# Attention with three score buffers, outputs in their free columns, and the grouped heads four jobs at a time with V stationary

## The chip, the cores and the metric

The kernel runs on one core of a Trainium2 chip. The metric is the device time of one execution in microseconds (us). The kernel before took 1500.85 us in the median of three runs (1499.09 to 1501.25).

## The reference

The reference is one layer of a diffusion backbone for 512 latent tokens and 128 prompt tokens of width 1024. What is touched here is the attention of two kinds of heads and the projections right behind it:

```python
def diff_attention(q, k, v, lam, lambda_init, subln_g):      # A: 8 heads, two maps each
    s = jnp.einsum('bqhnd,bkhnd->bhnqk', qb, k) * scale
    p = jax.nn.softmax(s, axis=-1)
    a = p[:, :, 0] - lam * p[:, :, 1]
    o = jnp.einsum('bhqk,bkhe->bqhe', a, v)
    o = rms_norm(o, subln_g) * (1.0 - lambda_init)
def gqa_attention(q, k, v):                                  # B: 16 query heads, 4 key/value heads
    s = jnp.einsum('bqhgd,bkhd->bhgqk', qg, k) * scale
    o = jnp.einsum('bhgqk,bkhd->bqhgd', jax.nn.softmax(s, axis=-1), v)
merged = sigmoid(ga) * (o_a @ w_br_a) + sigmoid(gb) * (o_b @ w_br_b)
x = ln_affine(alpha * x + g1 * (merged @ w_o), ...)
```

Latent queries attend to 640 keys (512 latent and 128 cached ones), prompt queries to the 128 prompt keys. Behind it come a router, an expert layer with two experts a token, and a second norm.

## The kernel before, in words

The kernel is written with five hand-ordered instruction streams, one for each engine, that meet at semaphores. Every engine works its own stream strictly in the order of the program. The stages are: modulation and the combined projection (to about 485 us), the attention (to about 811 us), the branch and output projections, the router, the experts, and the last norm.

**The attention.** A job is one tile of 128 queries with one head; its number is j. Heads come in 12 bundles: 8 of kind A (5 jobs, one for each query tile, two score maps a job) and 4 of kind B (4 query heads that share keys and values, times 5 tiles, one map a job), together 120 jobs and 160 maps. A job is wide for the four latent tiles (640 keys) and narrow for the prompt tile (128 keys). A job passes these steps:

- TensorE multiplies queries and keys into a score buffer of PSUM (`scores`, L1621; matmuls on L1633). There are two score buffers, `pair[0]` and `pair[1]`, used in turn (`spair`, L385); a map waits until the exponential of the map two before is done.
- VectorE takes the negated maximum of each row (L1186), and ScalarE the exponential with its row sum into an SBUF buffer `pbuf` (L874).
- For A, VectorE forms the difference of the two maps, with the reciprocals of the sums and lambda in it (L1196 to L1198).
- TensorE turns the 128x128 blocks of P into `pair[2]` (`turn_p`, L1636, L1643). There is one such place, so the turning waits until the job before has been copied out.
- ScalarE copies the turned P to SBUF (`copy_turned`, L397, the copy on L404); for one B job in three VectorE does it (`copied_by_dve`, L394).
- TensorE multiplies the turned P, as the stationary operand, with V (`times_v`, L1646, L1656) into one of two places in `pair[3]` (`obank`, L388).
- VectorE scales the output by the reciprocal sum into a staging tile (L1209, L1213), and GpSimd's queue stores a bundle's outputs, in rows of tokens, to DRAM (L1910).

The order in which each engine meets these steps is fixed by loops over j. TensorE's loop (L1659) and ScalarE's (L864) are

```python
for j in range(NJ + 3):                       # TensorE, L1659
    if j < NJ: scores(jobs[j][4])
    if 0 <= j - 2 < NJ: turn_p(j - 2)
    if j < NJ and not jobs[j][1]: scores(jobs[j][4] + 1)
    if 0 <= j - 3 < NJ: times_v(j - 3)
for j in range(NJ + 2):                       # ScalarE, L864: exponentials of job j, then
    if 2 <= j and not copied_by_dve(j - 2): copy_turned(act, act.copy, j - 2)
```

VectorE's loop (L1180) holds, for each j: the maxima of job j, the difference of job j-1 (A), its copy of job j-2 if it has one, and the scaling of the output of job j-4. SP's queue loads queries, keys and V of the bundles ahead, with two buffers; a load of V waits until the bundle two before is through its V products.

**Behind the attention.** The outputs are read back in rows of tokens, one query tile at a time, five tiles of A and then five of B (`load_o`, L879, three places). A's are squared (`square`, L889, ScalarE), normed per head (`norm_o`, L1216, VectorE, a chain of small steps with two passes of 1024 columns) and all ten are turned by TensorE (`turn_o`, L1678, transposes on L1675). ScalarE rounds the turned rows to the high part (`round_o`, L896), VectorE takes the low part (`rest_o`, L1228), and then the branch projection of the tile runs with three passes (`three_passes`, L1691, L1695 to L1697), 20 units v of 24 matmuls. The gain of the sub-norm is loaded by GpSimd's queue after the last store, and VectorE scales it.

The modulation earlier in the kernel uses matmuls whose stationary operand has 32 columns, in four column groups in turn (L1542).

## Time and profile before

| | us |
|---|---|
| median of the runs shown | 1500.85 (1499.09 to 1501.25) |
| the profiled execution's own time | 1499.63 |
| its span, first to last instruction | 1497.4 |
| TensorE busy in the span | 1300.7 |
| VectorE busy | 989.6 |
| ScalarE busy | 649.3 |
| GpSimd busy | 171.7 |
| mean granted TensorE clock | 0.935 of 2.4 GHz |

The engines are named PE (TensorE matmuls), PEld (its weight loads, beside the matmuls), DVE (VectorE), ACT (ScalarE), POOL (GpSimd) and SP (SyncE); ACTq and the like are their DMA issues. L12 is line 12 of the kernel. Busy time does not count waiting, and an instruction's duration reaches from its start to its end, so that pipelined instructions of TensorE overlap: the distance from one start to the next says how long the engine was held. What an idle engine waited for is inferred from semaphores.

### The profile page before, as it was taken

What the parts mean: (1) busy time and instruction counts of PE and PEld (TensorE: products, weight loads), DVE (VectorE), ACT (ScalarE), POOL (GpSimd) and SP (SyncE); (2) the same over time, 40 slices, a digit from 0 to 9 for tenths busy, and PEclk for the clock granted to TensorE, in tenths of its full rate; (3) what the DMA queues carried; (4) which work ended last, traced back from release to release, by engine and by line L of the source; (5) the groups of instructions that cost most, each with busy time, mean ns of one, the idle gap of its engine ahead of it and who ended that gap; (6) DMA issues with size and microseconds to landing.
All of it is one profiled execution on the core that took longest, in us unless ns stands there. A gap on an engine that the chain in (4) does not pass through costs nothing.

```text
span 1497.4 us, 20859 instructions
## 1 busy us (share of the span) xinstructions
PE 1300.7 (87%) x6836; PEld 1063.8 (71%) x6836; DVE 989.6 (66%) x1814; ACT 649.3 (43%) x962; POOL 171.7 (11%) x236
## 2 busy tenths in 40 slices
PE   6899999999999778799986799996389999999940
PEld 3677777667887667788886688785368888888830
DVE  3655521838561777755555844499689999999936
ACT  2422222323222566545553322200357888888812
POOL 0012111111122000000000000100101121112201
PEclk9799999999999899999998799997589999999975
DMA  9856554453535676602202434436489999999834
GB/s 354 268 183 218 190 211 162 155 183 102 183 134 172 160 181 173 172 26 61 80 19 69 160 121 137 146 137 243 166 301 354 364 383 388 391 391 375 312 149 70
DMA packets 144419, 301.05 MB, mean 201 GB/s; under 512 B 18972, under 2 KB 24636, under 8 KB 144344
## 3 DMA queue, kind: packets, MB, share of 16 engines
q1 hardware_dynamic: 122104, 232.19, 45.1%
q0 software_dynamic: 20800, 62.63, 13.1%
q10 hardware_dynamic: 1440, 5.24, 1.1%
q8 instruction: 45, 0.74, 0.2%
q14 instruction: 30, 0.25, 0.1%
HBM read 258.69 MB, written 53.90 MB: 209 GB/s over the span
## 4 chain that ended last, share of the span: by engine, by line
PE 73%; DVE 14%; issue 6%; ACT 4%; DMA 2%; SPq 1%; POOL 0%; ACTq 0%; DVEq 0%; POOLq 0%
PE psum_pair L1556 7%; PE psum_pair L1557 7%; PE psum_pair L1558 7%; PE psum_pair L1777 5%; PE psum_pair L1778 5%; PE psum_pair L1779 5%; PE psum_pair L1695 4%; PE psum_pair L1643 4%; PE psum_pair L1696 4%; PE psum_pair L1697 4%; PE psum_pair L1656 4%; PE psum_pair L1633 4%; PE psum_pair L1792 2%; PE psum_pair L1793 2%; PE psum_pair L1794 2%
## 5 line engine op out<-in xcount | busy, mean ns | idle before, releaser
L1556 PE MATMUL psum_pair<-w_parts,h_hi 128*128 128x512 f32 x520 | 209.9, 404 | 6.3 <-DVE h_lo L1164 6.3
L1557 PE MATMUL psum_pair<-w_parts,h_hi 128*128 128x512 f32 x520 | 205.5, 395 | 0.0
L1558 PE MATMUL psum_pair<-w_parts,h_lo 128*128 128x512 f32 x520 | 205.4, 395 | 0.0
L1186 DVE TENSOR_REDUCE minus_max<-psum_pair 128x1 f32<-128x640 f32 (+1 forms) x160 | 114.3, 715 | 99.0 <-PE psum_pair L1633 98.6
L874 ACT ACTIVATE p_unnormed<-psum_pair,minus_max 128x640 f32<-128x640 f32 (+1 forms) x160 | 113.5, 709 | 144.4 <-DVE minus_max L1186 144.2
L1022 DVE TENSOR_TENSOR w_parts<-w_raw,w_parts 128x1024 fp32r<-128x1024 f32 x72 | 83.3, 1220 | 106.1 <-ACT w_parts L789 106.0
L1633 PE MATMUL psum_pair<-k_bundle,q_bundle 128*128 128x512 f32 (+1 forms) x576 | 128.4, 342 | 5.8 <-ACT p_unnormed L874 5.1
L1656 PE MATMUL psum_pair<-v_bundle,p_turned 128*128 128x64 f32 (+1 forms) x1008 | 131.3, 275 | 0.0
L1556 PEld LDWEIGHTS psum_pair<-w_parts,h_hi 128*128 128x128 f32 x520 | 99.2, 191 | 37.4 <-issue 18.3
L1656 PEld LDWEIGHTS psum_pair<-v_bundle,p_turned 128*128 128x128 f32 x1008 | 122.9, 193 | 1.4
L1558 PEld LDWEIGHTS psum_pair<-w_parts,h_lo 128*128 128x128 f32 x520 | 99.3, 191 | 21.5
L1557 PEld LDWEIGHTS psum_pair<-w_parts,h_hi 128*128 128x128 f32 x520 | 99.5, 191 | 19.0
L1633 PEld LDWEIGHTS psum_pair<-k_bundle,q_bundle 128*128 128x128 f32 x576 | 89.0, 195 | 13.8 <-issue 6.8
L1435 DVE TENSOR_TENSOR w_parts<-w_raw_b,w_parts 128x1024 fp32r<-128x1024 f32 x76 | 88.0, 1220 | 4.3 <-ACT w_parts L951 4.3
L1435 DVE TENSOR_TENSOR w_parts<-w_raw,w_parts 128x1024 fp32r<-128x1024 f32 x76 | 87.8, 1217 | 0.6 <-ACT w_hi_c L951 0.6
L1435 DVE TENSOR_TENSOR w_lo_c<-w_raw_c,w_hi_c 128x1024 fp32r<-128x1024 f32 x76 | 87.8, 1216 | 0.2 <-ACT w_hi_c L951 0.2
L789 ACT CAST w_parts<-w_raw 128x1024 fp32r<-128x1024 f32 x72 | 70.3, 1047 | 40.3 <-PE psum_pair L1697 38.1
L800 ACT ACTIVATE turned_staging<-psum_pair 128x1024 f32<-128x1024 f32 (+1 forms) x38 | 36.4, 960 | 108.0 <-PE psum_pair L1588 108.0
L951 ACT CAST w_hi_c<-w_raw_c 128x1024 fp32r<-128x1024 f32 x76 | 73.7, 1047 | 7.6 <-DVE control L1426 7.6
L1695 PE MATMUL psum_pair<-w_parts,oA_turned_hi 128*128 128x512 f32 x160 | 66.0, 413 | 9.4 <-DVE oA_turned_lo L1232 7.9
L951 ACT CAST w_parts<-w_raw 128x1024 fp32r<-128x1024 f32 x76 | 74.0, 1051 | 0.2 <-issue 0.2
L951 ACT CAST w_parts<-w_raw_b 128x1024 fp32r<-128x1024 f32 x76 | 73.9, 1053 | 0.0
(311 smaller groups left out, 2585.0 us busy)
## 6 DMA issues: line engine op xcount, KB each, us to landing
w_raw<-in_w_gate_up SPq DMA_DIRECT2D x76, 512.0 KB, 7.6
w_raw_c<-in_w_gate_up SPq DMA_DIRECT2D x72, 512.0 KB, 8.6
w_raw_b<-in_w_down SPq DMA_DIRECT2D x72, 512.0 KB, 7.7
w_raw<-in_w_in SPq DMA_DIRECT2D x52, 512.0 KB, 8.8
ada_raw<-in_w_ada SPq DMA_DIRECT2D x32, 512.0 KB, 7.1
k_bundle<-k_transposed SPq DMA_DIRECT2D x28, 384.0 KB, 8.2
q_transposed<-turned_staging POOLq DMA_DIRECT2D x20, 512.0 KB, 4.0
ada_raw_early<-in_w_ada SPq DMA_DIRECT2D x16, 512.0 KB, 8.2
```

Source lines behind the costliest of these rows:

```text
L874: act.activation(pbuf[:, m % PR, 0:w], spair(m)[:, 0:w], ACT.Exp, bias=nmax[:, m % RR:m % RR + 1], accum_out=rsum[:, m % RR:m % RR + 1]).t ...
L951: act.copy(expert_hi(place, c), landing(place, c)).then_inc(hi_done, 1)
L1022: dve.tensor_tensor(w_parts[b % 2][:, 1, c], w_raw[:, c], w_parts[b % 2][:, 0, c].bitcast(F32), ALU.subtract).then_inc(lo_done, 1)
L1186: dve.tensor_reduce(nmax[:, m % RR:m % RR + 1], spair(m)[:, 0:width(j)], AX.X, ALU.max, negate=True).then_inc(nb_done, 1)
L1435: dve.tensor_tensor(expert_lo(place, c), landing(place, c), expert_hi(place, c).bitcast(F32), ALU.subtract).then_inc(lo_done, 1)
L1556: pe.matmul(bank(n), a_hi, hi, start=first, stop=False)
L1557: pe.matmul(bank(n), a_hi, lo, start=False, stop=False)
L1558: last = pe.matmul(bank(n), a_lo, hi, start=False, stop=end)
L1633: last = pe.matmul(spair(m)[:, c0:c0 + w], q, k[:, g, k0:k0 + w], start=g == 0, stop=g == 1)
L1656: last = pe.matmul(obank(j)[:, 0:w], ptb[:, j % 2, k], vb[bi % 2][:, vt, 0:w], start=k == 0, stop=k == len(tiles) - 1)
L1695: pe.matmul(out, a_hi[:, kk], hi, start=kk == 0, stop=False)
L1777: pe.matmul(out, xt_hi[:, kk], hi, start=kk == 0, stop=False)
```

## The change

Score maps get three buffers in turn (`scores_of`). Outputs go to free columns of a score buffer: the output of a job (A) or group (B) is put behind the 640 score columns of a later map, its host, and ScalarE takes it after that map's exponential (`take_o`). In A, the V product of job j-3 is issued before the second scores of job j. In B, P is scaled by the reciprocal sum before it is turned, four jobs (two query tiles times two heads) share one V product with V as the stationary operand and 256 columns streaming, the two heads at output partitions 0 to 63 and 64 to 127, and the output comes out turned; it is stored turned and needs no transposes later. VectorE copies one B job in five instead of one in three. The read-back and first norm of A's outputs stand inside B's loops. The diff, cut:

```diff
-        pair = [... for i in range(4)]
+        psum = ctx.enter_context(nc.psum_tensor("psum_pair", [P, 8 * CW], F32))
+        pair = [psum[:, 2 * CW * i:2 * CW * (i + 1)] for i in range(4)]
...
-        for bi, (kind, _) in enumerate(bundles):
-            for r in range(REP if kind else 1):
-                for tt in range(NT):
+            together = [[(r, tt) for tt in tts for r in (2 * half, 2 * half + 1)] for half in range(REP // 2)
+                        for tts in ((0, 1), (2, 3), (PROMPT,))] if kind else [[(0, tt)] for tt in range(NT)]
...
+        for g, (_, kind, members) in enumerate(outs):
+            j = members[-1] + (4 if kind else 3)
+            host[g] = (jobs[j][4] + (0 if jobs[j][1] else 1)) if j < NJ else NM + j - NJ
+            hosted[host[g]] = g
...
-        def spair(m):
-            return pair[m % 2]
+        def scores_of(m):
+            return pair[m % SR][:, 0:NKEY]
+        def out_of_map(m, w):
+            return pair[m % SR][:, NKEY:NKEY + w]
...
         def copied_by_dve(j):
-            return jobs[j][1] == 1 and j % 3 == 0
+            return jobs[j][1] == 1 and (j - N_A) % 5 == 2
...
+            # ScalarE
+            def take_o(g):
+                act.wait_ge(pv_ready, g + 1)
+                if kind:
+                    act.copy(ost_b[:, q % 2, 0:w], out_of_map(host[g], w)).then_inc(o_out, 1)
+                else:
+                    act.activation(ost[:, bi % 2, tt], out_of_map(host[g], P), ACT.Copy,
+                                   scale=rinv[:, m % RR:m % RR + 1]).then_inc(o_out, 1)
+            for j in range(NJ + 4):
+                if j < NJ:
+                    for m in [m for m in range(jobs[j][4], NM) if maps[m][0] == j]:
...
+                        act.activation(pbuf[:, m % PR, 0:w], scores_of(m)[:, 0:w], ACT.Exp, ...
+                        if m in hosted:
+                            take_o(hosted[m])
+                if 2 <= j < NJ + 2 and not copied_by_dve(j - 2):
                     copy_turned(act, act.copy, j - 2)
+                if j == N_A + 20:
+                    for z in range(OS):
+                        load_o(z)
+                if j == N_A + 30:
+                    square(0)
+                if j == N_A + 50:
+                    square(1)
...
+            # VectorE: the maxima of job j, then for i = j - 1
+                    if kind:
+                        link(dve.reciprocal(rinv[:, s0:s0 + 1], rsum[:, s0:s0 + 1]))
+                        dve.tensor_scalar(p, p, rinv[:, s0:s0 + 1], None, ALU.mult).then_inc(a_done, 1)
+                    dve.wait_ge(a_done, i + 1)
+                i = j - 2
+                if 0 <= i < NJ and copied_by_dve(i):
+                    copy_turned(dve, dve.tensor_copy, i)
+                if j == N_A + 40:
+                    norm_o(0)
...
+            norm_o(1)
...
+            # TensorE
+            def wait_place(m):
+                if m >= SR:
+                    pe.wait_ge(e_done, min(m - SR + 1, NM))
+                    if m - SR in hosted:
+                        pe.wait_ge(o_out, hosted[m - SR] + 1)
...
+            def times_v(g):
...
+                    if kind:
+                        w = len(members) // 2 * P
+                        for half in range(2):
+                            last = pe.matmul(out_of_map(host[g], w)[HD * half:HD * half + HD], vb[bi % 2][:, vt, 0:HD],
+                                             ptb_b[:, g % 2, half, k, 0:w], start=first, stop=end)
...
-            for j in range(NJ + 3):
-                if j < NJ:
+            for j in range(NJ + 4):
+                if j < NJ and not jobs[j][1]:
                     scores(jobs[j][4])
-                if 0 <= j - 2 < NJ:
-                    turn_p(j - 2)
-                if j < NJ and not jobs[j][1]:
+                    if 0 <= j - 2:
+                        turn_p(j - 2)
+                    if 0 <= j - 3:
+                        times_v(j - 3)
                     scores(jobs[j][4] + 1)
-                if 0 <= j - 3 < NJ:
-                    times_v(j - 3)
+                else:
+                    if j - 3 < N_A:
+                        times_v(j - 3)
+                    if N_A <= j - 4 < NJ and outs[out_of[j - 4]][2][-1] == j - 4:
+                        times_v(out_of[j - 4])
+                    if j < NJ:
+                        scores(jobs[j][4])
+                    if j - 2 < NJ:
+                        turn_p(j - 2)
...
             def turn_o(z):
-                if z >= 2 * NT:
+                if z >= NT:
                     return
...
+            # GpSimd's queue, for each of B's 24 groups
+                pool.wait_ge(o_out, g + 1)
+                pool.dma_start(ot_scr[2 * bundles[bi][1] + r // 2, :, tt * P:tt * P + w], ost_b[:, q % 2, 0:w]).then_inc(ob_st[q % 2], 16)
```

B's outputs are then loaded turned (in pieces of 128 columns, 512 bytes), ScalarE rounds and VectorE splits them straight from SBUF.

## Rows read from the trace of the kernel before

**Rows 1.** Windows: length; busy PE, PEld, DVE, ACT, POOL (count); granted clock; DMA share, GB/s.

```profile
485.00:631.50 146.50, 117.11 (x803) 102.91 (x804) 112.10 (x242) 85.61 (x205) 6.57 (x8) 0.97 0.66 169
631.50:811.10 179.60, 161.60 (x1288) 149.69 (x1286) 101.07 (x265) 89.64 (x210) 3.45 (x4) 1.00 0.16 45
811.10:825.70 14.60, 1.94 (x8) 1.57 (x8) 6.38 (x20) 3.23 (x3) 3.57 (x6) 0.54 0.64 205
825.70:842.60 16.90, 10.26 (x41) 8.19 (x41) 14.72 (x34) 8.02 (x8) 0.00 (x0) 0.70 0.35 122
```

**Rows 2.** Timeline in A: start, duration, engine, line; in brackets the idle time before.

```profile
550.39 0.35 DVE L1213 TENSOR_SCALAR o_staging<-psum_pair,p_sums_recip 128x128 f32<-128x128 f32 x1
...
550.75 0.74 PE L1643 MATMUL psum_pair<-identity,p_difference 128*128 128x128 f32 x5 [0.92 <-ACT p_turned L404]
...
551.25 0.88 PE L1633 MATMUL psum_pair<-k_bundle,q_bundle 128*128 128x512 f32 x4
...
551.97 1.33 PE L1656 MATMUL psum_pair<-v_bundle,p_turned 128*128 128x128 f32 x10
552.17 0.82 DVE L1186 TENSOR_REDUCE minus_max<-psum_pair 128x1 f32<-128x640 f32 x1 [0.70 <-PE psum_pair L1633]
...
553.03 0.80 ACT L874 ACTIVATE p_unnormed<-psum_pair,minus_max 128x640 f32<-128x640 f32 x1 [0.64 <-DVE minus_max L1186]
553.05 0.42 PE L1633 MATMUL psum_pair<-k_bundle,q_bundle 128*128 128x128 f32 x2
...
553.81 0.68 ACT L404 COPY p_turned<-psum_pair 128x640 f32<-128x640 f32 x1
...
554.64 0.74 PE L1643 MATMUL psum_pair<-identity,p_difference 128*128 128x128 f32 x5 [1.17 <-ACT p_turned L404]
```

**Rows 3.** Order of instructions in B.

```profile
800.72 0.88 PE L1633 MATMUL psum_pair<-k_bundle,q_bundle 128*128 128x512 f32 x4
...
801.63 0.82 DVE L1186 TENSOR_REDUCE minus_max<-psum_pair 128x1 f32<-128x640 f32 x1 [0.91 <-PE psum_pair L1633]
...
802.49 0.80 ACT L874 ACTIVATE p_unnormed<-psum_pair,minus_max 128x640 f32<-128x640 f32 x1 [1.44 <-DVE minus_max L1186]
...
803.28 0.68 ACT L404 COPY p_turned<-psum_pair 128x640 f32<-128x640 f32 x1
...
804.11 0.73 PE L1643 MATMUL psum_pair<-identity,p_unnormed 128*128 128x128 f32 x5 [1.10 <-ACT p_turned L404]
```

**Rows 4.** Groups by shape, whole span: busy us, mean ns of one.

```profile
L874 ACT ACTIVATE p_unnormed<-psum_pair,minus_max 128x128 f32<-128x128 f32 x32 | 11.8, 368 | 19.9 <-DVE minus_max L1186 19.9
...
L1186 DVE TENSOR_REDUCE minus_max<-psum_pair 128x1 f32<-128x128 f32 x32 | 9.3, 289 | 22.0 <-PE psum_pair L1633 21.7
...
L404 ACT COPY p_turned<-psum_pair 128x128 f32<-128x128 f32 x19 | 4.9, 257 | 0.5 <-PE psum_pair L1643 0.5
...
L1153 DVE TENSOR_SCALAR x_tiles<-x_tiles,x_mean_var,x_rstd 128x1024 f32<-128x1024 f32 x5 | 3.7, 808 | 0.0
```

**Rows 5.** TensorE's order in the modulation stage.

```profile
35.99 3.64 PE L1542 MATMUL psum_pair<-ada_raw_early,cond_columns 128*32 128x512 f32 x32
```

**Rows 6.** Order behind the attention, VectorE and TensorE.

```profile
814.76 1.22 DVE L1221 TENSOR_REDUCE o_mean_squares<-o_squares 128x8 f32<-128x1024 f32 x1 [3.06 <-ACT o_squares L894]
...
818.43 1.22 DVE L1225 TENSOR_TENSOR o_rows<-o_rows,o_rms_recip 128x1024 f32<-128x1024 f32 x1
...
819.91 1.94 PE L1675 MATMUL psum_pair<-identity,o_rows 128*128 128x128 f32 x8 [8.94 <-DVE o_rows L1225]
...
875.76 1.03 PE L1675 MATMUL psum_pair<-identity,o_rows 128*128 128x128 f32 x8
876.57 0.47 PE L1695 MATMUL psum_pair<-w_parts,oB_turned_hi 128*128 128x512 f32 x1
```

**Rows 7.** Window of a stretch at the attention's start.

```profile
498.50:502.00 3.50, 3.47 (x16) 3.13 (x15) 2.00 (x4) 1.97 (x5) 0.00 (x0) 0.56 0.38 85
```

**Rows 8.** Timeline: a V pass in that stretch.

```profile
499.45 2.34 PE L1656 MATMUL psum_pair<-v_bundle,p_turned 128*128 128x128 f32 x10
```

More of the change, by code:

```diff
@@ L367, in hybrid_step @@
                     maps += [(j, 0)] if kind else [(j, 0), (j, 1)]
-        NJ, NM = len(jobs), len(maps)
-        job_end = {bi: max(j for j, q in enumerate(jobs) if q[0] == bi) + 1 for bi in range(len(bundles))}
+                    out_of.append(len(outs))
+                outs.append((bi, kind, list(range(first, len(jobs)))))
+        NJ, NM, N_OUT = len(jobs), len(maps), len(outs)
+        N_A = NT * A_HEADS
+        host, hosted = {}, {}
+        for g, (_, kind, members) in enumerate(outs):
+            j = members[-1] + (4 if kind else 3)
+            host[g] = (jobs[j][4] + (0 if jobs[j][1] else 1)) if j < NJ else NM + j - NJ
+            hosted[host[g]] = g
+        out_end = {bi: max(g for g, q in enumerate(outs) if q[0] == bi) + 1 for bi in range(len(bundles))}
         map_end = {bi: max(m for m, q in enumerate(maps) if jobs[q[0]][0] == bi) + 1 for bi in range(len(bundles))}
@@ L1632, in scores @@
                     for k0, c0, w in runs:
-                        last = pe.matmul(spair(m)[:, c0:c0 + w], q, k[:, g, k0:k0 + w], start=g == 0, stop=g == 1)
+                        last = pe.matmul(scores_of(m)[:, c0:c0 + w], q, k[:, g, k0:k0 + w], start=g == 0, stop=g == 1)
                 last.then_inc(s_ready, 1)
@@ L1649, in times_v @@
                 if bi:
                     pe.wait_ge(v_in[bi % 2], 32 * ((bi + 1) // 2))
-                if j >= 2:
-                    pe.wait_ge(o_out, j - 1)
-                tiles = [PROMPT] if tt == PROMPT else list(range(TL)) + [NT]
-                w = HD if kind else P
+                wait_place(host[g])
+                tiles = [PROMPT] if jobs[last_job][3] == PROMPT else list(range(TL)) + [NT]
                 for k, vt in enumerate(tiles):
-                    last = pe.matmul(obank(j)[:, 0:w], ptb[:, j % 2, k], vb[bi % 2][:, vt, 0:w], start=k == 0, stop=k == len(tiles) - 1)
+                    first, end = k == 0, k == len(tiles) - 1
+                    if kind:
+                        w = len(members) // 2 * P
+                        for half in range(2):
+                            last = pe.matmul(out_of_map(host[g], w)[HD * half:HD * half + HD], vb[bi % 2][:, vt, 0:HD], ptb_b[:, g % 2, half, k, 0:w], start=first, stop=end)
+                    else:
+                        last = pe.matmul(out_of_map(host[g], P), ptb_a[:, g % 2, k * P:(k + 1) * P], vb[bi % 2][:, vt, 0:P], start=first, stop=end)
@@ L1670, in _ @@
+            pe.wait_ge(o_out, N_OUT)
             pe.wait_ge(e_done, NM)
+            for i in range(2):
+                pe.wait_ge(pt_full[i], NJ // 2)
             def turn_rows(n, src):
@@ L1706, in _ @@
                 pe.wait_ge(lo_done, NC_CH * (b + 1))
[L1707 removed]
+                if v < NT:
                     pe.wait_ge(tr_free[(TR_O + v) % 2], (TR_O + v) // 2 + 1)
+                elif v < 2 * NT:
+                    pe.wait_ge(ot_done, v - NT + 1)
                 cols = slice(tt * P, (tt + 1) * P)
```

233 lines of the change are left out of this document (121 added, 112 removed).

## The prediction, made before the change was run

> **What bounds the kernel now.** I read the windows by stage first, then the order of single instructions inside the attention, because the change lives there. In the window table the attention of the differential heads (A) takes 146.5 us and that of the grouped heads (B) 179.6 us; then come 14.6 and 16.9 us in which TensorE works little before the branch projections run steadily [rows 1]. No engine is full in A: TensorE is busy 117 of 146.5 us, VectorE 112, ScalarE 86. In B TensorE is busy 162 of 180. So A must be bound by a chain, B partly.
>
> The chain in A shows in the order of instructions [rows 2]. Call J a job; a wide one has 640 keys, a narrow one (prompt) 128, in the ratio 4 to 1. The transposes of job J-2 start at 550.75. 0.50 us later TensorE starts the second score pass of J (551.25), then V of J-3 (551.97). The maximum follows its scores by 0.92 (552.17), the exponential the maximum by 0.86 (553.03), ScalarE's copy of the turned J-2 by 0.78 (553.81), and the transposes of J-1, which need that one PSUM place, by 0.83 (554.64). The sum is 3.89 us, and 554.64 - 550.75 is 3.89. The copy could run earlier, but stands behind both exponentials of J in ScalarE's queue, and the transposes wait for it. The V pass lies outside the chain: issued after the second scores, it covers TensorE's wait. With 32 wide jobs of 3.89 and 8 narrow ones at about 1.7 this makes some 138 us; the 9 left of 146.5 are the start.
>
> B has the same chain with one map a job [rows 3]: scores 800.72, maximum 801.63, exponential 802.49, copy 803.28, transposes of the job before 804.11, that is 3.39 us from the scores of J to the transposes of J-1. With 0.50 for these transposes, scores of J+2 cannot start before 3.89 plus whatever TensorE does between.
>
> **Part 1, A: V moves ahead of the second scores.** The new order on TensorE is first scores J, transposes J-2, V of J-3, second scores J. V now stands inside the chain: 551.97 to the next scores at 553.05 is 1.08 us for ten instructions [rows 2]. VectorE's scaling of the output goes; ScalarE takes the output instead, after the exponential of the hosting map and before the copy, again in the chain. The nearest row is the 128x128 copy of 0.257 us [rows 4]; its bounds are 0 (if it hid) and 0.37, the narrow exponential [rows 4]; I take 0.26, a copy of the same size. The cycle becomes 3.89 + 1.08 + 0.26 = 5.23 us. A narrow job adds 0.22 (two of ten V instructions) and 0.26. Per head 4 x 1.34 + 0.5 = 5.8 us, for eight heads **+46 us**. VectorE's saving of 0.35 a job is worth nothing, since VectorE waits for scores. The third score buffer is worth nothing: each pass waits behind earlier work of TensorE, not for a buffer, and the copy's place behind the exponentials is unchanged. Were the chain shorter, that buffer would be what TensorE waits for next.
>
> **Part 2, B: V stationary.** Four jobs share one V pass of 5 key tiles x 2 halves x 2 instructions = 20, each over 256 columns. Ten instructions over 128 columns took 1.08 us, so one over 256 costs 0.22; one half is ten, 2.2 us. Whether the halves run side by side B's rows don't show; other rows do: 32 instructions with 32 columns of the array each, four such groups in turn, 512 columns streamed, take 3.64 us, 0.114 each [rows 5], where one after another 512 columns would take 0.43. So I take 2.2 us a group (20 x 0.11 for the weights gives the same), with 4.4 as the other end. The Trainium skill ("TensorE: Matmul & The Clock Gate", Measured speedup vs the span model) gives three column tiles a speedup of only 2.38; by that as an estimate a group would cost 2.8 us and the sum 9 us more. The 0.114 above speaks for nearly full overlap.
> Sixteen wide groups are 35 us against 64 x 1.08 = 69 now, so 34 us of TensorE's work go. But where does the pass stand? Before the scores of the job four after the group's last member: numbers 1, 7, 11, 17 of a bundle's 20, and 3 and 13 for the prompt groups. All are odd, and the chain links J to J+2. So the chain through the odd jobs carries every V pass whole. Per bundle: ten steps of 3.89 = 38.9; the two narrow odd jobs, the two narrow copies and the two narrow transposes are shorter by 1.4 + 0.4 + 0.4 each [rows 2, 4], -4.5; four wide passes with the taking of 256 columns, 4 x (2.2 + 0.35), where 0.35 lies between the copies of 128 and of 640 columns, 0.26 and 0.68 [rows 2, 4], +10.2; two narrow ones, +1.4. That is 46.0, four bundles 184 us, against 179.6: **+4**. Today VectorE copies one job in three, right after its maximum and ahead of the chain's end; after the change one in five, behind the normalisation, so that relief goes too and is in the 46.0.
> The new scaling of P (640 elements) I bound by 0.35 below (a 128-column scaling) and 0.82 above (the 640-wide maximum) [rows 2]; the scaling of 1024 elements took 0.81 [rows 4], so about 0.5. It costs nothing: VectorE is busy 101 of 180 us in B [rows 1], and the transposes that wait for it come two jobs later. Without that cover it would cost 64 x 0.65 = 42 us.
> Moved into B: the first norm block, 814.76 to 819.65 = 4.9 us of VectorE [rows 6], in front of the next maximum; two squares of some 1.1 and three DMA issues on ScalarE. I take **+7** (between 0, in idle time, and 10). GpSimd's queue gets 24 small stores in place of 4; a staging place comes up again eight jobs later, over 16 us: nothing.
>
> **Part 3, after the attention.** TensorE idled 8.9 us for the first norm [rows 6]. That norm is done beforehand and the second runs on VectorE while TensorE finishes its last transposes and V: **-9**, of 14.6. In the next stretch VectorE is busy 14.7 of 16.9 us [rows 1]; one block of 4.9 leaves it: **-5**. The turned rows of B need no transposes: five times 0.81 (875.76 to 876.57) [rows 6] is **-4**. Their loads come in 512-byte pieces and have three places in turn: nothing; if a load were late, TensorE would wait at the first B projection.
>
> **Sum.** +46 +4 +7 -18 = +39 on the profiled execution's 1499.6 us; the median shown is 1.2 above it: about 1540 us. Its own range, from the bounds of the takes, the norm block and the overlap after the attention, is 1525 to 1558. A measurement of this kernel can tell about 0.2%, 3 us, from no change.
>
> **Rivals.**
> *Side by side fails* (0.12). The halves run one after another: 16 x 2.2 = +35, 1575 us. Against it stand rows 5; for it, that those show 32-column groups, not 64.
> *The clock falls* (0.13). TensorE would work 3.0 of each 5.2 us in A. At the attention's start the granted clock was 0.56 in one stretch, mostly the lower level of 1.2 GHz, and a V pass took 2.34 instead of 1.33 us [rows 2, 7, 8]; between the stalls after the attention it averaged 0.54 and 0.70 [rows 1]. With TensorE's 2.5 us of the cycle longer by 1.76 times, a cycle grows by 1.9; if half the cycles do so, 16 x 1.9 = +30, 1570 us. The Trainium skill ("TensorE: Matmul & The Clock Gate", The HAM clock gate) holds that idle gaps put the clock back to 1.2 GHz; in A now, with waits of 0.9 us, it stays at 0.97.
> *TensorE's work decides* (0.10, the other side). With three score buffers the scores run ahead, the copy finds its exponentials done, and the stages shrink to TensorE's work: A 117 us, B 162 - 72 + 39 = 129, and -18: 29 + 51 + 18 = -98, 1402 us. The place is the transposes' wait for the copy; it decides if in A one job's transposes follow the last by under 3.9 us. Against it: the queue order on both engines ties the second scores of J to the transposes of J-2 whatever the buffers.
> *V in A is covered after all* (0.05): only the takes stay, 1499.6 + 11 + 11 - 18, about 1504 us.
>
> **Numbers.** The forecast has 0.60, giving 1540. Leaving out the last two rivals (0.15), the range takes in the others: 1582 is the first rival with the forecast's upper bounds in part, 1512 the forecast's low end if half of A's V pass, 17 us, hides and the other terms stand near their middle. Faster is the third rival and a sliver of the fourth, 0.11; within 0.2% 0.03; slower 0.86.
>
> **What would show it.** Right: wide A jobs at 5.2 us between transposes, TensorE idle about 2.2 us before each and released by ScalarE's copy; stage A near 193 us. B near 190, waits by the same copy, V passes of 2.2 us with starts 0.11 apart. First branch matmul some 6 us after the attention. Wrong: an A cycle at or under 3.9 us; a V group over 3 us; a wait for the normalised P ahead of the transposes; a granted clock near half in A.

## The result and the profile after the change

The changed kernel takes **1591.8 us** (median of 4 runs, 1591.0 to 1594.6) against 1500.5 on the same chip: a ratio of 1.061, 95% interval 1.0595 to 1.0632. It is slower by 91 us. The forecast of 1540 us had the direction; the time lies 10 us above the top of its range.

The windows by stage, as [rows 1] show them for the kernel before (length; busy PE, PEld, DVE, ACT, POOL with counts; granted clock; DMA share and GB/s):

```profile
485.00:708.50 223.50, 148.01 (x804) 132.55 (x805) 102.59 (x206) 93.93 (x243) 6.56 (x8) 0.82 0.45 114
708.50:923.20 214.70, 155.49 (x966) 113.41 (x964) 122.82 (x281) 100.12 (x247) 16.06 (x25) 0.87 0.14 43
```

Stage A went from 146.5 to 223.5 us (+77.0), stage B from 179.6 to 214.7 (+35.1). The rest of the span behind them went from 1497.4 - 811.1 = 686.3 to 1589.3 - 923.2 = 666.1 (-20.2). The three make the +91.9 of the spans. The third number from the end is the new thing: the granted clock was 0.97 in A and 1.00 in B, and is 0.82 and 0.87. In B TensorE has a quarter fewer instructions and is busy 155.5 us, hardly less than its 161.6 before.

TensorE's waits in the changed kernel (line that waited, releaser: us in all, times, longest):

```profile
PE psum_pair L1702 <- ACT p_turned_a L427: 67.5, 37, 2.5
PE psum_pair L1702 <- ACT p_turned_b L431: 52.3, 39, 3.0
```

The transposes (L1702) wait for ScalarE's copy of the turned block, as the prediction had it; no single wait is long. One cycle of A, the counterpart of [rows 2]:

```profile
561.22 0.74 PE L1702 MATMUL psum_pair<-identity,p_difference 128*128 128x128 f32 x5 [1.12 <-ACT p_turned_a L427]
...
561.80 1.28 PE L1721 MATMUL psum_pair<-v_bundle,p_turned_a 128*128 128x128 f32 x10
...
562.84 1.57 PE L1692 MATMUL psum_pair<-k_bundle,q_bundle 128*128 128x512 f32 x8
563.76 0.82 DVE L1290 TENSOR_REDUCE minus_max<-psum_pair 128x1 f32<-128x640 f32 x1 [1.91 <-PE psum_pair L1692]
...
564.62 0.79 ACT L958 ACTIVATE p_unnormed<-psum_pair,minus_max 128x640 f32<-128x640 f32 x1 [1.85 <-DVE minus_max L1290]
...
565.41 0.36 ACT L947 ACTIVATE o_staging<-psum_pair,p_sums_recip 128x128 f32<-128x128 f32 x1
565.65 0.69 ACT L427 COPY p_turned_a<-psum_pair 128x640 f32<-128x640 f32 x1
...
566.49 0.30 PE L1702 MATMUL psum_pair<-identity,p_difference 128*128 128x128 f32 x1 [2.09 <-ACT p_turned_a L427]
```

Transposes, V pass, the second scores, maximum, exponential, the taking, the copy, the next transposes: 566.49 - 561.22 = 5.27 us, where 5.23 was predicted. That is a cycle at the upper of TensorE's two levels. Not all are. The same two lines a little later, on TensorE alone:

```profile
575.30 0.74 PE L1702 MATMUL psum_pair<-identity,p_difference 128*128 128x128 f32 x5 [2.07 <-ACT p_turned_a L427]
...
581.81 0.74 PE L1702 MATMUL psum_pair<-identity,p_difference 128*128 128x128 f32 x5 [2.34 <-ACT p_turned_a L427]
...
586.20 1.30 PE L1702 MATMUL psum_pair<-identity,p_difference 128*128 128x128 f32 x5 [0.53 <-ACT p_turned_a L427]
587.29 2.34 PE L1721 MATMUL psum_pair<-v_bundle,p_turned_a 128*128 128x128 f32 x10
593.22 0.38 PE L1702 MATMUL psum_pair<-identity,p_difference 128*128 128x128 f32 x1 [2.08 <-ACT p_turned_a L427]
```

A cycle that lies at the lower level (1.2 GHz) lasts 593.22 - 586.20 = 7.02 us; V takes 2.34 instead of 1.28 and the five transposes 1.30 instead of 0.74. One that changes level midway took 581.81 - 575.30 = 6.51. In B it looks like this (TensorE's transposes L1702, V passes L1719 and one score pass L1692):

```profile
826.54 0.74 PE L1702 MATMUL psum_pair<-identity,p_unnormed 128*128 128x128 f32 x5 [0.85 <-ACT p_turned_b L431]
827.21 2.38 PE L1719 MATMUL psum_pair<-p_turned_b,v_bundle 128*64 128x256 f32 x20
...
833.25 0.74 PE L1702 MATMUL psum_pair<-identity,p_unnormed 128*128 128x128 f32 x5 [2.11 <-ACT p_turned_b L431]
...
836.66 0.30 PE L1702 MATMUL psum_pair<-identity,p_unnormed 128*128 128x128 f32 x1 [0.42 <-DVE p_turned_b L431]
...
842.52 1.30 PE L1702 MATMUL psum_pair<-identity,p_unnormed 128*128 128x128 f32 x5 [1.66 <-ACT p_turned_b L431]
...
853.03 0.74 PE L1702 MATMUL psum_pair<-identity,p_unnormed 128*128 128x128 f32 x5 [0.86 <-ACT p_turned_b L431]
853.70 2.38 PE L1719 MATMUL psum_pair<-p_turned_b,v_bundle 128*64 128x256 f32 x20
856.01 0.90 PE L1692 MATMUL psum_pair<-k_bundle,q_bundle 128*128 128x512 f32 x4
...
859.74 1.30 PE L1702 MATMUL psum_pair<-identity,p_unnormed 128*128 128x128 f32 x5 [2.11 <-ACT p_turned_b L431]
...
864.28 0.45 PE L1702 MATMUL psum_pair<-identity,p_unnormed 128*128 128x128 f32 x1
864.66 3.21 PE L1719 MATMUL psum_pair<-p_turned_b,v_bundle 128*64 128x256 f32 x20
...
871.12 0.74 PE L1702 MATMUL psum_pair<-identity,p_unnormed 128*128 128x128 f32 x5 [1.66 <-ACT p_turned_b L431]
...
875.79 0.73 PE L1702 MATMUL psum_pair<-identity,p_unnormed 128*128 128x128 f32 x5 [1.55 <-ACT p_turned_b L431]
...
879.82 0.74 PE L1702 MATMUL psum_pair<-identity,p_unnormed 128*128 128x128 f32 x5 [0.85 <-ACT p_turned_b L431]
```

Ten jobs make half a bundle: 853.03 to 879.82 is 26.8 us. Its steps of two jobs each are 6.71 (to 859.74, with a V pass), 4.54, 6.84 (with the second V pass, at the lower clock in part), 4.67 and 4.03. The two steps that were slowed have twins at the upper level half a bundle earlier: 833.25 to 836.66 is 3.41 and 836.66 to 842.52 is 5.86. With them the half bundle would be 24.7 us. A pass of 20 instructions takes 2.38, or 3.21 where the clock changes within it.

Behind the attention the first branch matmul comes 3.8 us after the windows' mark at 923.2, where 14.6 passed before [rows 1, 6], and the first projection of B's outputs waits only 1.54 us for its operand:

```profile
926.99 0.47 PE L1767 MATMUL psum_pair<-w_parts,oA_turned_hi 128*128 128x512 f32 x1 [2.69 <-DVE oA_turned_lo L1253]
...
970.43 0.47 PE L1767 MATMUL psum_pair<-w_parts,oB_turned_hi 128*128 128x512 f32 x1 [1.54 <-DVE oB_turned_lo L1257]
```

### The profile page after: what moved, and what is told of

The parts are those of the page before. It is cut to its first block, busy times and chain, and to the rows that moved or that the text cites. A ratio compares the mean times of both kernels' runs of the same rounds, so it can differ in the third digit from the quotient of the medians.

```text
span 1589.3 us, 20107 instructions
## 1 busy us (share of the span) xinstructions
PE 1315.6 (83%) x6476; PEld 1048.6 (66%) x6476; DVE 993.1 (62%) x1764; ACT 665.5 (42%) x1036; POOL 183.5 (12%) x256
## 4 chain that ended last, share of the span: by engine, by line
PE 72%; DVE 13%; issue 6%; ACT 6%; DMA 2%; SPq 1%; POOL 0%; DVEq 0%; ACTq 0%; POOLq 0%
PE psum_pair L1610 6%; PE psum_pair L1611 6%; PE psum_pair L1612 6%; PE psum_pair L1702 5%; PE psum_pair L1851 5%; PE psum_pair L1852 4%; PE psum_pair L1853 4%; PE psum_pair L1692 4%; PE psum_pair L1721 4%; PE psum_pair L1767 3%; PE psum_pair L1768 3%; PE psum_pair L1769 3%; DVE minus_max L1290 3%; PE psum_pair L1719 3%; PE psum_pair L1866 2%
## 5 line engine op out<-in xcount | busy, mean ns | idle before, releaser
L1692 PE MATMUL psum_pair<-k_bundle,q_bundle 128*128 128x512 f32 (+1 forms) x576 | 137.4, 375 | 1.3 <-ACT value_staging L847 0.7
L1692 PEld LDWEIGHTS psum_pair<-k_bundle,q_bundle 128*128 128x128 f32 x576 | 102.4, 224 | 17.9 <-issue 8.0
L1702 PE MATMUL psum_pair<-identity,p_unnormed 128*128 128x128 f32 x336 | 59.4, 308 | 58.4 <-ACT p_turned_b L431 52.3
L1702 PE MATMUL psum_pair<-identity,p_difference 128*128 128x128 f32 x168 | 32.4, 329 | 68.9 <-ACT p_turned_a L427 67.5
L1702 PEld LDWEIGHTS psum_pair<-identity,p_unnormed 128*128 128x128 f32 x336 | 41.2, 156 | 71.7 <-DVE p_unnormed L1302 42.2
```

Source lines behind the costliest of these rows:

```text
L1692: last = pe.matmul(scores_of(m)[:, c0:c0 + w], q, k[:, g, k0:k0 + w], start=g == 0, stop=g == 1)
L1702: last = pe.transpose(turned_p()[:, k * P:(k + 1) * P], src[:, k * P:(k + 1) * P], ident[:])
```

## The experiments

Stage lengths are read from the window view, split at the first transposes of B and at the end of the attention. The kernels of experiments 1 to 6 ran once each, those of 7 to 12 four times. Where a kernel ran once, differences of some microseconds within a stage are not read.

**1. V ahead of the second scores, alone, in the kernel before.** The diff, on TensorE's queue:

```diff
+                if 0 <= j - 3 < N_A:
+                    times_v(j - 3)
                 if j < NJ and not jobs[j][1]:
                     scores(jobs[j][4] + 1)
-                if 0 <= j - 3 < NJ:
+                if N_A <= j - 3 < NJ:
                     times_v(j - 3)
```

> The kernel before with one edit: in A the V pass of job j-3 stands ahead of the second scores of job j, everything else as before. Theory: the cycle of a wide job in A rises from 3.89 by the 1.08 us of the pass to 4.97 at the full clock, that is 36 us, and the clock falls as TensorE waits more, which adds 0 to 25 us; A 183 to 207 us, B unchanged at 180, total 1536 to 1560 us. Rival (the position is covered, the loss is in the buffers or in the taking): within 5 us of 1500.

Measured: 1559.4 us. Stage A:

```profile
484.90:690.50 205.60, 143.44 (x808) 125.82 (x807) 112.15 (x242) 86.69 (x207) 7.09 (x9) 0.85 0.48 123
```

Stage A grew by 59 us and B stayed (179.5). The passes alone, 32 x 1.08 and 8 x 0.22, give 36. Part of the other 23 is the clock of 0.85: TensorE's same instructions are busy 143 us instead of 117. Part is a longer chain: the transposes now also wait 15.0 us for VectorE's difference of the maps, 2.5 before. How the 23 divide was not measured. The order of V in A costs more than the length of its passes.

**2. The same place undone in the changed kernel**: outputs in two banks of their own, so that V can stand behind the second scores again, and two score buffers.

```diff
-        PR, RR, SR = 4, 16, 3
+        PR, RR, SR = 4, 16, 2
...
-            return pair[m % SR][:, NKEY:NKEY + w]
+            return pair[3][:, CW * (hosted[m] % 2):CW * (hosted[m] % 2) + w]
...
+                    scores(jobs[j][4] + 1)
                     if 0 <= j - 3:
                         times_v(j - 3)
-                    scores(jobs[j][4] + 1)
```

> The changed kernel with two score buffers instead of three, outputs in two PSUM banks of their own, and in A the V pass behind the second scores again. Theory (V stands in A's chain): the cycle from one job's transposes to the next falls from 5.27 at the full clock to about 4.15 us (the taking of the output stays in it), the granted clock in A rises from 0.82 to about 0.95, stage A falls from 223 to about 160 us, B stays near 215; total about 1528 us. Rival (the third buffer helps, and A's loss is the taking by ScalarE or the fallen clock alone): A stays above 200 us and the total above 1570.

Measured: 1537.2 us.

```profile
484.90:654.20 169.30, 125.65 (x805) 109.61 (x806) 102.69 (x206) 96.68 (x245) 6.56 (x8) 0.91 0.59 152
654.20:869.00 214.80, 156.13 (x966) 113.62 (x964) 123.08 (x281) 100.14 (x247) 15.81 (x25) 0.87 0.14 43
```

A falls by 54 us, to 169.3 where about 160 was expected; the clock's rise from 0.82 to 0.91 is part of it. B, where only the buffers changed and no order, is 214.8 against 214.7: there the third buffer is worth nothing, as predicted. In A buffers and order changed together, so for A this run alone does not show it.

**3. And B's V pass behind the scores.** On top of experiment 2:

```diff
+                    if j < NJ:
+                        scores(jobs[j][4])
                     if j - 3 < N_A:
                         times_v(j - 3)
                     if N_A <= j - 4 < NJ and outs[out_of[j - 4]][2][-1] == j - 4:
                         times_v(out_of[j - 4])
-                    if j < NJ:
-                        scores(jobs[j][4])
```

> The changed kernel with the outputs in two banks of their own and the V pass of stage A behind the second scores (as measured before: 1537 us, stage B 214.8), and now stage B's V pass between the scores and the transposes instead of ahead of both. Theory (a pass ahead of the scores is carried whole by the chain scores, maximum, exponential, copy; behind the scores it runs while VectorE and ScalarE work): 16 passes x 2.2 us less what still shows, so stage B 180 to 195, and 1502 to 1517 us in all. Rival (stage B is set by the copy at the end of ScalarE's turn alone, wherever the pass stands): stage B 205 to 215.

Measured: 1492.8 us. Its stages:

```profile
484.90:645.90 161.00, 120.39 (x805) 105.41 (x806) 102.95 (x207) 96.85 (x245) 6.56 (x8) 0.96 0.61 158
645.90:825.00 179.10, 135.34 (x966) 100.23 (x964) 120.48 (x281) 102.49 (x247) 14.13 (x25) 0.98 0.17 53
```

B lost 35.7 us, against the rival, which had it at 205 or more: the chain carried V. That 16 passes of 2.2 also make 35 is in part luck. The clock went from 0.87 to 0.98 in the same step and gave some of the 35.7 back, so the passes need not have left the chain whole; how the sum divides was not measured. The kernel is now at about the time of the one before, below the expected 1502 because A came out at 161.0 instead of 169.3, with the very same instructions and orders in A and a clock of 0.96 instead of 0.91. So a stage of two kernels, alike in all its instructions, can differ by some 8 us from one execution to another, and the clock moves with it.

**4. B's V pass issued twice**, in the changed kernel.

```diff
-                for k, vt in enumerate(tiles):
+                for k, vt in [(k, vt) for _ in range(2 if kind else 1) for k, vt in enumerate(tiles)]:
```

> The changed kernel with the V pass of each group in stage B issued twice (the same products again into the same sums, started anew, so nothing else changes). Theory of the prediction (every pass of stage B is carried whole by the chain): 16 passes x 2.3 us and the four of stage A's kind untouched, about +37 to +45 us on 1592, stage B 214.7 to about 250 to 258, less what a higher granted clock gives back (at clock 1.0 the stage's own work would be 0.13 x 155 = 20 us shorter, so the least is about +17). Rival (the passes are hidden, and stage B is set by the copy alone): stage B within 5 us of 214.7.

Measured: 1632.1 us, +40.

```profile
708.20:964.80 256.60, 197.04 (x1318) 140.80 (x1316) 122.93 (x281) 100.14 (x247) 16.06 (x25) 0.87 0.12 36
```

B grew by 41.9 us while TensorE's busy time in it grew by 41.5. Every microsecond of V stands on the path, and this run shows it with the clock unchanged. More work did not raise the mean clock here.

**5. TensorE kept busy**, in the changed kernel: products of the identity with itself ahead of the transposes, written to the next score buffer and overwritten later; eight a job in A, four in B.

```diff
+            def fill(m, n):
+                if m + 1 < NM:
+                    wait_place(m + 1)
+                    for _ in range(n):
+                        pe.matmul(scores_of(m + 1)[:, 0:P], ident[:], ident[:], start=True, stop=True)
...
                     scores(jobs[j][4])
+                    fill(jobs[j][4], 8)
```

> The changed kernel with products of the identity with itself put into TensorE's waits ahead of the transposes: 8 a job in A (1.7 us), 4 in B (0.9 us); nothing reads them. Theory (two losses: the chain, and a clock that falls because TensorE waits in it): the granted clock rises from 0.82 and 0.87 to 0.97 or more, A goes from 223 to about 193 us at a cycle of 5.25, B from 215 to about 192; total about 1540 us although TensorE has more work. Rival (the clock costs nothing on the chain): the total rises or stays, 1590 us or more.

Measured: 1560.0 us, 32 less than the changed kernel, though over the expected 1540, with 1281 instructions more on TensorE (two to a product). The last row is one bundle of A:

```profile
484.90:686.10 201.20, 187.28 (x1477) 176.34 (x1476) 103.40 (x207) 95.45 (x246) 7.09 (x9) 1.00 0.50 128
686.10:891.00 204.90, 198.44 (x1574) 170.41 (x1572) 119.91 (x281) 100.33 (x247) 14.14 (x25) 0.99 0.15 46
571.26:594.96 23.70, 22.52 (x179) 21.32 (x180) 12.53 (x26) 11.58 (x30) 0.86 (x2) 1.00 0.50 126
```

The clock is back at 1.00 and 0.99, and the stages lose 22.3 and 9.8 us although nothing in their chains was shortened. That is the direct test of the clock: useless work in the waits pays. It is a lower bound of the clock's price, since the fillers in part exceed the waits: TensorE is now busy 187 of 201 us.

A closer figure for A leaves out its start, where the fillers run before there is a wait to fill. Inside the bundle shown the transposes still wait for the copy, and the wide cycle is 5.26 us (571.26 to 576.52), as in the changed kernel at the upper level. From the transposes of the second job to the first of B, in the changed kernel and in this one:

```profile
495.82:708.51 212.69, 140.50 (x771) 126.57 (x772) 94.82 (x192) 88.25 (x230) 6.02 (x7) 0.82 0.43 110
```

```profile
500.16:686.10 185.94, 172.71 (x1372) 163.18 (x1372) 95.52 (x193) 88.38 (x230) 6.01 (x7) 1.00 0.48 124
```

They differ by 26.8 us, about 27: that is what the clock takes in A.

**6. The copy ahead of the exponentials**, in the changed kernel: between the two exponentials in A, ahead of the exponential in B.

```diff
+            def copy_of(j):
+                if 2 <= j < NJ + 2 and not copied_by_dve(j - 2):
+                    copy_turned(act, act.copy, j - 2)
...
             for j in range(NJ + 4):
+                if j >= NJ or jobs[j][1]:
+                    copy_of(j)
                 if j < NJ:
                     for m in [m for m in range(jobs[j][4], NM) if maps[m][0] == j]:
+                        if m > jobs[j][4]:
+                            copy_of(j)
                         act.wait_ge(nb_done, m + 1)
...
-                if 2 <= j < NJ + 2 and not copied_by_dve(j - 2):
-                    copy_turned(act, act.copy, j - 2)
```

> The changed kernel with ScalarE's copy of the turned P moved forward: in A between the two exponentials of a job, in B ahead of the exponential. Theory (the copy behind the exponentials closes the chain): in A the next longest chain is VectorE's difference, which stands behind the second maximum, 4.6 us a wide job at the full clock, A about 172 to 190 us; in B the chain is gone and TensorE's 1.9 us a job decide, about 150 us; total about 1480 us. Rival (the transposes wait for the normalised P or for scores, not for the copy): less than 15 us are gained.

Measured: 1503.9 us, 88 less than the changed kernel.

```profile
484.90:655.90 171.00, 117.13 (x809) 101.99 (x808) 102.62 (x206) 96.74 (x244) 7.10 (x9) 0.98 0.58 148
655.90:836.00 180.10, 139.97 (x966) 102.92 (x965) 124.12 (x281) 102.17 (x250) 16.61 (x25) 0.96 0.18 54
```

Its waits name what comes next:

```profile
PE psum_pair L1708 <- DVE p_difference L1314: 51.4, 38, 1.9
PE psum_pair L1708 <- DVE p_unnormed L1308: 19.0, 22, 3.5
...
PE psum_pair L1708 <- DVE p_turned_b L431: 12.5, 15, 1.4
```

A, 171.0, came out just under the expected 172 to 190, with VectorE's difference as the next wait, as expected. B was expected near 150 and was 180.1, and the time lies 24 us over the expected 1480: with the copy early, the transposes wait for VectorE's scaled P and for VectorE's own copies, and the V pass still stands ahead of the scores. The clock rose to 0.98 and 0.96, so the 88 us hold the clock as well as the chain.

**7. The copy ahead of the exponentials, alone, in the kernel before** (the same edit; its loop runs to NJ + 2).

> The kernel before, with one thing changed: ScalarE copies the turned block of the job two back ahead of its work on the new job in stage B, and between the two exponentials in stage A, instead of behind the exponentials. Theory (in the changed kernel and in the kernel before alike, the copy at the end of ScalarE's turn is what TensorE waits for): stage A falls from 146.5 to about 133 us (the next chain is VectorE's, 3.5 us a job) and stage B from 179.6 to 150 to 165; the time is 1455 to 1480. Rival: the early copy only pays where V stands in the way, so that the kernel before gains nothing: 1495 to 1505 us.

Measured: 1469.8 us against 1500.8, ratio 0.979, interval 0.978 to 0.981.

```profile
484.90:623.60 138.70, 117.13 (x808) 102.14 (x807) 112.15 (x242) 83.52 (x206) 7.12 (x9) 0.98 0.70 179
623.60:782.80 159.20, 157.33 (x1288) 148.92 (x1286) 100.59 (x264) 90.95 (x212) 3.45 (x4) 1.00 0.18 52
```

One instruction moved in ScalarE's queue takes 31 us off the kernel before. B is then TensorE's work, busy 157.3 of 159.2 us; A lost 7.8 us instead of the 13 expected; the time lies in the expected 1455 to 1480.

**8. All orders altered**, in the changed kernel: experiments 2 and 3 and the early copy, except that a job of B that hosts a V pass keeps its exponential first:

```diff
+                hosts = N_A <= j < NJ and jobs[j][4] in hosted
+                if j >= NJ or (jobs[j][1] and not hosts):
+                    copy_of(j)
```

> The changed kernel with all of the orders altered: outputs in two banks of their own (two score buffers), the V pass of stage A behind the second scores, that of stage B between the scores and the transposes, and ScalarE's copy early (in a stage B job that hosts a V pass, behind the exponential). Theory (the saved TensorE work counts once the orders let it): stage A about 135 to 145 us, stage B 150 to 165, the granted clock at 0.97 or more in both; with the 17 us gained behind attention 1430 to 1455. Rival (the lower TensorE work by itself draws the clock down, whatever the order): clock under 0.93 in A or B and a time above 1475.

Measured: 1466.3 us, ratio 0.977, interval 0.975 to 0.979. A 138.9 us at clock 0.99, and B:

```profile
623.80:799.20 175.40, 139.40 (x969) 101.71 (x968) 123.10 (x281) 102.93 (x247) 14.44 (x26) 0.97 0.19 55
```

The clock is held, against the rival. But the time is 11 us over the expected 1430 to 1455: B is 175.4 where 150 to 165 was expected, longer than the 159.2 of experiment 7 although TensorE has 18 us less to do in it. Its longest waits are still for ScalarE's copy:

```profile
PE psum_pair L1709 <- ACT p_turned_b L431: 25.8, 33, 4.3
```

**9. VectorE's difference between the two maxima of A**, on top of experiment 8.

```diff
-                    for m in [m for m in range(jobs[j][4], NM) if maps[m][0] == j]:
...
+                    row_max(j, jobs[j][4])
                 i = j - 1
...
                     dve.wait_ge(a_done, i + 1)
+                if j < NJ and not jobs[j][1]:
+                    row_max(j, jobs[j][4] + 1)
```

> The kernel with all of the orders altered (run just before this one), and in stage A VectorE takes the difference of the job before between the two maxima of the new job, instead of behind both. Theory: the difference then comes one maximum (about 0.65 us) earlier for the transposes that wait for it, but the second maximum and its exponential come later; a gain of 5 to 11 us in stage A if the wait for the difference ends the idle time, 0 or a loss of up to 10 us if the chain goes through the second exponential. Stage B unchanged.

Measured: 1461.9 us, ratio 0.974, interval 0.972 to 0.975. Stage A went from 138.9 to 132.8 us, a gain within the expected 5 to 11, and B stayed (175.6).

**10. Two buffers for the turned block**, in the changed kernel. The third pair of banks goes to the transposes; outputs lie in the free columns of the turned buffer whose copy is done; V is issued last in both stages; ScalarE's copy stays late.

```diff
-        PR, RR, SR = 4, 16, 3
+        PR, RR, SR = 4, 16, 2
...
-        def turned_p():
-            return pair[SR][:, 0:NKEY]
+        def turned_p(j):
+            return pair[2 + j % 2][:, 0:NKEY]
...
-                if j:
-                    pe.wait_ge(pt_full[(j - 1) % 2], (j - 1) // 2 + 1)
+                if j >= 2:
+                    pe.wait_ge(pt_full[j % 2], j // 2)
+                n_out = len([g for g in range(N_OUT) if cycle_of(g) <= j + 1])
+                if n_out:
+                    pe.wait_ge(o_out, n_out)
```

> The changed kernel with the third pair of banks used otherwise: two score buffers and two buffers for the turned blocks, the outputs in the free columns of a turned buffer whose copy is done, the V pass last in each job in both stages, ScalarE's order left as it was (copy behind the exponentials). Theory (what TensorE waits for in the changed kernel is one turned buffer coming free): with two of them the waits for the copy go away although the copy stays late: stage A 130 to 140 us, stage B 145 to 165, time 1425 to 1455. Rival (ScalarE's and VectorE's work in each job is the limit, the buffer is not): stage B above 175 as with the altered orders, time 1460 or more.

Measured: 1481.0 us, ratio 0.987, interval 0.986 to 0.989: under the kernel before, but 26 us over the top of what was expected; B came out between the two expectations, A far above.

```profile
484.90:642.00 157.10, 119.61 (x811) 103.83 (x809) 102.71 (x206) 96.17 (x246) 7.10 (x9) 0.97 0.63 161
642.00:810.30 168.30, 136.75 (x955) 103.44 (x956) 118.70 (x270) 101.76 (x245) 15.70 (x24) 0.99 0.19 57
```

```profile
PE psum_pair L1706 <- ACT o_staging L952: 34.3, 31, 1.6
```

The wait for the copy went, and a new one took its place in A: the output lies in a turned buffer, and ScalarE takes it last in its turn, so the transposes wait for that. In B, with one taking in four jobs, the second buffer is worth 7 us against experiment 8.

**11. The same with the difference between the maxima.**

> As the run before it (two turned buffers), and in stage A VectorE takes the difference between the two maxima. Theory: with the copy off the chain, the difference for the transposes comes one maximum (0.8 us) earlier, a gain of up to 5 us in stage A, as it was 6 us with one turned buffer; rival: stage A is now set by TensorE's own 117 us and VectorE's 103, so that the order changes nothing (within 2 us).

Measured: 1484.1 us (1481.5 to 1487.2), no gain; A 161.3 us at a clock of 0.94. With the taking as the chain, the difference earlier is worth nothing. The case lies nearer the rival, though what sets A is the taking and not TensorE's work.

**12. A from experiment 9, B from experiment 10.** Turned block in one buffer and outputs in banks of their own in A, two turned buffers in B:

```diff
+            return pair[2 + (j % 2 if jobs[j][1] else 0)][:, 0:NKEY]
...
+            if not outs[g][1]:
+                return pair[3][:, CW * (g % 2):CW * (g % 2) + w]
+            return pair[2 + (cycle_of(g) - 3) % 2][:, NKEY:NKEY + w]
```

> Two versions joined: stage A as in the version with all orders altered and the difference between the maxima (one turned buffer, outputs in two banks of their own, ScalarE's copy between the exponentials; 132.8 us there), stage B as in the version with two turned buffers (168.3 us there, ScalarE's copy behind the exponential, outputs in a turned buffer that is copied). Theory (the stages add, and the two turned buffers hurt only stage A, where the taking of each output ended ScalarE's turn and held up the next transposes for 34 us): stage A 131 to 136, stage B 166 to 170, time 1450 to 1460, under the 1461.9 of the best version so far. Rival (the gain of two turned buffers in stage B was a matter of how the stage is entered or of the clock in that run): stage B 174 or more, 1460 to 1466 in all.

Measured: **1456.3 us**, ratio 0.971, interval 0.969 to 0.972, the best version here; it beats the kernel before by 44 us and the changed one by 136.

```profile
484.90:618.00 133.10, 116.88 (x810) 102.51 (x809) 103.70 (x207) 94.20 (x245) 6.94 (x9) 0.97 0.75 191
618.00:785.00 167.00, 135.72 (x946) 102.61 (x946) 117.60 (x268) 101.77 (x245) 16.03 (x24) 0.99 0.19 58
```

```profile
PE psum_pair L1716 <- DVE p_unnormed L1311: 15.6, 23, 1.0
...
PE psum_pair L1716 <- ACT o_turned_staging L950: 8.1, 16, 3.4
```

The stages add up as expected: 133.1, 167.0 and the time all lie in the ranges named. Its attention takes 300.1 us, experiment 7's 297.9 with the old V; the whole gain over experiment 7, 13.6 us, lies behind the attention, where this form is 15 us shorter (1454.7 - 785.0 = 669.7 against 1467.9 - 782.8 = 685.1). In B itself V stationary has gained nothing, 167.0 us against 159.2: VectorE is busy 118 us instead of 101, and TensorE waits for P scaled by VectorE and, in 16 places, for ScalarE's taking of the output.

## Why the prediction was right and wrong

**Right: the mechanism of A.** V in the chain makes a cycle of 5.27 us where 5.23 was written, with the taking at 0.24 (565.41 to 565.65) where 0.26 stood. Experiment 1 shows the place of V alone, by adding it; experiment 2 undoes it together with the buffers. The third score buffer was worth nothing in B (experiment 2); for A that stays argued. A whole bundle of A grew a little more than was summed: 17.41 us before (550.75 to 568.16), 23.70 at the full clock (experiment 5), so 6.3 where 5.8 was written and 50 us where +46 stood.

**Right: V in B runs side by side and is carried whole.** 20 instructions lie between 853.70 and the next scores at 856.01, 2.31 us where 2.2 was written; experiment 4 (+41.9 for 41.5 of work, at the same clock) shows that all of it is on the path. Experiment 3 agrees in direction. The Trainium skill ("TensorE: Matmul & The Clock Gate", Measured speedup vs the span model) gives three column tiles a speedup of 2.38, from which the prediction made an estimate of 2.8 us a group; the trace, with two tiles of 64 columns, stands at 2.31, nearer to full overlap.

**Right: behind the attention**, -20.2 where -18 was summed; its three parts were not measured one by one.

**Wrong: the clock.** This is the step that failed. The prediction took the forecast's sum at full clock in both stages, without a term for it, held "the clock falls" for a rival at 0.13, and sized it at half of A's cycles, +30, with B left out. All three choices failed in one direction. The price of one cycle was right: a cycle at the lower level measured 7.02, which is 5.27 + 1.75, where 1.9 was written. In A it came to about 27 us (experiment 5), near the rival's +30. B fell as well, to 0.87: the two slowed steps above cost (4.54 - 3.41) + (6.84 - 5.86) = 2.1 us in one half bundle of eight, so some 10 to 17 us in the stage, with experiment 5's 9.8 as the lower bound. What in the profile of before spoke against it, "in A now, with waits of 0.9 us, it stays at 0.97", was a reading at another length of wait: the waits about doubled, from 0.92 and 1.17 to 2.09 us in a cycle of 5.27. The stretch at 0.56 [rows 7] was a warning that the stage could run at the lower level, though TensorE was busy all through it and it did not show what brings the level down. With less TensorE work and a longer chain in both stages, the forecast had to ask what becomes of the clock in both.

The Trainium skill ("TensorE: Matmul & The Clock Gate", A second HAM failure mode: psum-queue depth-cycling) tells of a clock that goes to and fro because TensorE idles briefly and often between groups of matmuls. The trace agrees: A's longest wait before the transposes was 2.5 us and its mean clock 0.82. The prediction had cited from that page only what it says of idle gaps.

**Wrong in size: B's chain at full clock.** 46.0 us a bundle was written, 23.0 a half; the trace gives 24.7, put together from its steps at the upper level: eight times 1.7 = 14 us more in all. The passes (5.1) and ten jobs of 1.945 (19.45) with 0.7 for the prompt pass make 25.2; so of the 2.2 us that the narrow jobs were to save, only about 0.5 shows. 3.41 and 5.86 us are 0.5 to 0.6 under their wide twins (3.89 and 6.44), and the steps of 6.71, 4.67 and 4.03 are 0.1 to 0.3 over theirs (6.44, 4.59 with the prompt pass, 3.89). The moved norm block was put at +7; the half bundle in which it lies, 798.30 to 827.21, is 28.9 us, 2 over the 26.8 that is usual for the others (25.7 to 27.3); in experiment 5 the half bundle with the norm block took 29.3 us at a clock of 0.94 and the next 25.6 at 1.00, 3.7 more. So the term was some 3 to 5 us too large.

The account of the miss, then. A, 31 us over its term: the clock 27, the chain 4. B, 24 over: the chain 14, the norm block -5 to -3, and the clock with what remains, 14 to 16. Behind the attention -2. B's clock is the least certain of them: it is a remainder, and lies between experiment 5's bound of 9.8 and the 17 of one half bundle times eight. In both stages together the clock is some 41 to 43 of the 52 us that were missed, and B's chain most of the rest.

**What became of the idea.** The change's own gains are real and were covered by its orders: with the orders altered (experiments 8 to 12) they show, but only behind the attention. TensorE's saving in B, 18 us by experiments 7 and 8, turns into waits for VectorE's scaling and ScalarE's work. The prediction turned down its rival "TensorE's work decides" for the right reason, the orders in the queues; experiment 7 shows that it needed no third buffer but one instruction moved in ScalarE's queue, and with that B of the kernel before does become TensorE's work.

Open: why the same stage A ran at a clock of 0.91 once and 0.96 once (experiments 2 and 3), how the 23 us of experiment 1 and the 35.7 of experiment 3 divide between chain and clock, and what share of B's last 167 us belongs to VectorE and what to ScalarE.

## What to carry to other kernels

When a wait goes up inside a cycle, price TensorE's clock with it: work out the cycle at either level and in every stage whose waits grow, and add it to the chain's term rather than keep it as a rival. Before giving a kernel more buffers, look at what the last instruction of each engine's turn releases: here a copy at the end of ScalarE's turn held both kernels, and moving it ahead of the exponentials was worth 31 us in one and 88, clock included, in the other. Work saved on an engine counts only where that engine's own work, and not a chain through it, sets the stage.

## What the runs showed of the hardware that was not expected

Useless matmuls can pay: 1281 more instructions on TensorE made the kernel 32 us faster, with the granted clock from 0.82 and 0.87 to 1.00 and 0.99. Many short waits brought the clock down with none over 3.0 us, and did so in two stages of different rhythm. Adding TensorE work inside the chain (experiment 4, B's V pass twice) did not raise it, 0.87 to 0.87, while filling the waits did. And stage A, instruction for instruction the same in two kernels, ran at a mean clock of 0.91 in one execution and 0.96 in another, 8 us apart.
